# Modulation halves in the first input product: one and a half per token tile's product in place of one

## The reference, cut to what matters

```python
for l in range(DEPTH):                                  # DEPTH = 2
    mod_l = (silu_c @ w_mod[l] + b_mod[l])[:, None, :]  # (1024) @ (1024, 6144)
    mod_c = (silu_cc @ w_mod[l] + b_mod[l])[None, None, :]
    ...                                                 # split into shift, scale, gate, twice
    h_l = rmsnorm(x_lat, norm_mix_pre[l]) * (1.0 + sc1_l) + sh1_l
    h_c = rmsnorm(x_ctx, norm_mix_pre[l]) * (1.0 + sc1_c) + sh1_c
    m_l, m_c = hybrid_mixer(h_l, h_c, ...)              # h @ w_in, then attention and an SSD scan, then @ w_out
    x_lat = x_lat + g1_l * rmsnorm(m_l, norm_mix_post[l])
    ...
```

## Time and profile before

| | |
|---|---|
| time, median of 3 runs | 2771.52 us (2766.29 to 2773.17) |
| the profiled execution | 2772.69 us, its span 2771.4 us |
| PE, DVE, ACT, POOL busy | 95%, 77%, 54%, 4% of the span |
| mean granted TensorE clock | 0.969 |
| input product of layer 0 | from 40 to 175 us |
| attention and scan of layer 0 | from 175 to 316 us |

### The profile page before, as it was taken

How to read it: one execution, slowest core, us unless ns; L and a number is a source line. 1 busy time by engine, 2 the same in 40 slices (tenths; PEclk the granted TensorE clock), 3 DMA queues, 4 the chain that set the end, 5 groups by cost and what they waited for, 6 DMA issues and landing times.

```text
span 2771.4 us, 32200 instructions
## 1 busy us (share of the span) xinstructions
PE 2620.0 (95%) x12954; PEld 2132.0 (77%) x12954; DVE 2125.7 (77%) x2511; ACT 1486.9 (54%) x1665; POOL 110.6 (4%) x145
## 2 busy tenths in 40 slices
PE   7989998998998889999999999999999999999997
PEld 4767676887777678877788777788888888888886
DVE  4555566787647657868688667799999999999997
ACT  4332364445443244344633526677667776767674
POOL 4023100000000300000000000000000000000000
PEclk9999899999999989999999999999999999999999
DMA  7543545885553036952289340599999999999994
GB/s 277 183 156 122 190 166 191 299 304 203 180 210 122 1 121 240 327 197 95 96 305 328 136 175 31 185 371 364 351 367 368 353 362 365 362 354 367 369 364 189
DMA packets 290442, 675.24 MB, mean 244 GB/s; under 512 B 16726, under 2 KB 113158, under 8 KB 271344
## 3 DMA queue, kind: packets, MB, share of 16 engines
q1 hardware_dynamic: 285152, 664.35, 65.9%
q0 software_dynamic: 4272, 7.72, 1.1%
q10 hardware_dynamic: 864, 1.06, 0.1%
HBM read 671.98 MB, written 1.10 MB: 243 GB/s over the span
## 4 chain that ended last, share of the span: by engine, by line
PE 76%; DVE 13%; ACT 7%; DMA 2%; issue 1%; SPq 0%; POOL 0%; ACTq 0%; DVEq 0%; POOLq 0%
PE psum L553 21%; PE psum L555 21%; PE psum L554 21%; PE psum L76 7%; DVE wslot_r L563 3%; PE psum L1524 1%; PE psum L396 1%; ACT whi_r L76 1%; PE psum L1663 1%; DVE cacc L76 1%; PE psum L3063 1%; DVE dslot_r L563 1%; DMA first<-in_w_mod 1%; PE psum L2091 1%; DVE x L76 1%
## 5 line engine op out<-in xcount | busy, mean ns | idle before, releaser
L553 PE MATMUL psum<-whi_r,xhi_r 128*128 128x512 f32 (+1 forms) x752 | 295.5, 393 | 12.0 <-DVE wslot_r L563 5.4
L563 DVE TENSOR_TENSOR wslot_r<-wslot,whi_r 128x2048 fp32r<-128x2048 f32 (+1 forms) x114 | 255.6, 2252 | 61.5 <-ACT whi_r L76 61.1
L555 PE MATMUL psum<-whi_r,xlo_r 128*128 128x512 f32 (+1 forms) x752 | 290.4, 386 | 0.0
L554 PE MATMUL psum<-wslot_r,xhi_r 128*128 128x512 f32 (+1 forms) x736 | 283.7, 385 | 0.0
L76 ACT ACTIVATE whi_r<-wslot 128x2048 fp32r<-128x2048 f32 (+1 forms) x114 | 212.6, 1878 | 50.8 <-DMA wslot<-in_w_up 19.5
L563 DVE TENSOR_TENSOR wslot_r<-wslot,arena_r 128x2048 fp32r<-128x2048 f32 x85 | 194.0, 2288 | 18.7 <-ACT arena_r L3022 18.1
L563 DVE TENSOR_TENSOR ring_r<-ring,wide_r 128x2048 fp32r<-128x2048 f32 x84 | 191.8, 2288 | 17.8 <-ACT wide_r L3022 16.6
L563 DVE TENSOR_TENSOR wslot_r<-wslot,wide_r 128x2048 fp32r<-128x2048 f32 x83 | 189.7, 2288 | 16.7 <-ACT wide_r L3022 16.3
L563 DVE TENSOR_TENSOR ring_r<-ring,arena_r 128x2048 fp32r<-128x2048 f32 x84 | 191.6, 2287 | 11.6 <-ACT arena_r L3022 10.8
L3022 ACT ACTIVATE arena_r<-wslot 128x2048 fp32r<-128x2048 f32 x85 | 162.3, 1917 | 68.6 <-PE psum L555 45.6
L3022 ACT ACTIVATE arena_r<-ring 128x2048 fp32r<-128x2048 f32 x84 | 160.5, 1918 | 69.3 <-PE psum L555 48.5
(11 more groups left out here) (540 smaller groups left out, 6334.5 us busy)
## 6 DMA issues: line engine op xcount, KB each, us to landing
wslot<-in_moe_w_gate SPq DMA_DIRECT2D x29, 2048.0 KB, 8.0
ring<-in_moe_w_down SPq DMA_DIRECT2D x29, 2048.0 KB, 8.3
dot<-in_w_dots SPq DMA_DIRECT2D x112, 512.0 KB, 6.1
wslot<-in_moe_w_up SPq DMA_DIRECT2D x28, 2048.0 KB, 8.5
ring<-in_moe_w_up SPq DMA_DIRECT2D x28, 2048.0 KB, 8.8
ring<-in_moe_w_gate SPq DMA_DIRECT2D x27, 2048.0 KB, 8.2
wslot<-in_moe_w_down SPq DMA_DIRECT2D x27, 2048.0 KB, 8.1
dslot<-in_w_mod SPq DMA_DIRECT2D x42, 1024.0 KB, 4.8
```

The costliest lines, as they stand in the source:

```text
L553: t.matmul(out_, hi, w_hi, start=start, stop=False)
L554: t.matmul(out_, hi, w_lo, start=False, stop=False)
L555: return t.matmul(out_, lo, w_hi, start=False, stop=stop)
L563: return v.tensor_tensor(one_pass(lo), src, one_pass(hi), ALU.subtract)
```

## The change

One number: behind the products of the first layer's input, each `fill` gives 1.5 steps in place of 1.

```diff
@@ -1445,7 +1445,7 @@
                     if n + 2 < len(order):
                         fetch_tile(order[n + 2])
                 if p_ != start:
-                    fill(2)
+                    fill(3 if l == 0 else 2)
                 between(j, p_)
```

## The result

The changed kernel takes 2784.28 us in the median of 7 runs (2775.68 to 2790.76), the kernel before 2770.81 (7 runs, 2766.29 to 2773.17). The ratio is 1.0039, its 95% interval 1.0021 to 1.0057: slower by 0.4%, some 11 us, where 2781 was forecast. The profiled execution took 2778.27, 5.6 above the profiled one of before.

What follows compares the result with a forecast made beforehand. PE was taken to bound the kernel, busy for 95% of 2771.4 us. Input product +10.2, mix -4.4 and end of the mix +4.3 gave +10.1 on the median of 2771.5: 2781 us, range 2766 to 2788.

Steps and rivals of the forecast that it cites:

- `col_mod` wait and its clock gone: Input product: the 4.20 us gap ahead of the third tile's first half goes, with its low clock: -6.9 us.
- KV's pairs: Input product, around KV: paired halves wait for their transfers, n19 4.4, n20 0.3 and n23 1.0 us.
- low clock behind KV's wait: Input product: the 4.4 us wait in KV brings the clock down behind it, 0.87 + 1.85 = 2.7 us.
- input product: Stretch from 40 to 175 us: 7.05 + 0.5 - 6.9 + 9.6 = +10.2 us (8.7 to 12).
- mix to the scan's end: Stretch from 175 to 291 us: smaller gaps, less low clock and fewer waits beside attention, -4.4 us (-2.6 to -6.2).
- end of the mix, to the output product: Behind the scan's end: without its seven halves attention runs at low clock, as in layer 1: +5.1 - 0.8 = +4.3 us.
- a gap of 4.4 is as long as that of 4.20, and so I give it the same loss by the clock: Input product, KV: n19's transfer wait loses as much by the clock as the old column wait, 2.7 us.
- 1.76 + 1.1: Mix: n26 fills the 1.76 us gap at 185.44, saving 1.0; the gap at 203.30 is over about 1.1 earlier.
- I take half, 1.8: Mix: of about 3.6 us lost to low clock behind the gap at 203.30, half is saved, 1.8.
- rival B: End of the mix keeps the full clock, turning +4.3 into -7.1: -1.3 in all, 2770 us, not slower; chance 0.2.
- f: Share of the end of the mix at 2.4 GHz; the total change goes as 10.1 - 11.4 f.
- Rival C: Transfers of n19 and n20 land in time for KV's second product, 7.4 us less: +2.7, 2774 us; chance 0.13.

Runs made afterwards that it cites:

- second profile: The changed kernel run again with no edit and profiled a second time: 2787.1 us, ratio 1.0061 to the kernel before.
- asked early: The changed kernel, each half asking for the transfer of the half after next right behind its own last matmul, not at the next step: ratio 1.0022 to the kernel before.
- no transfers: The changed kernel with the transfers of n8 to n39 left out, their matmuls reading what stands in the buffers: ratio 1.0034 to the kernel before.
- filled end: The changed kernel with bursts of matmuls that nothing reads between the steps of the mix's end: ratio 1.0041 to the kernel before.
- columns early: The kernel before with two steps in place of one behind Q's last product, so the second tile's columns stand ahead of KV: 2769.92 us, ratio 0.9992.
- bare end: The kernel before with six of the seven halves behind the scan's last product left out, matmuls and transfers: ratio 1.0003.
- KV single: The changed kernel with one step behind each of KV's products, as before the change: 2776.9 us, ratio 1.0014 to the kernel before.

## Why the prediction came out nearly right

The forecast of 2781 stood on +10.1. The ratio says +10.8, the medians differ by 13.5. Its terms did not come out equally well.

| term | predicted | measured in the profile |
|---|---|---|
| more matmuls in the input product | +7.05 | as counted |
| wait behind the third tile's columns | +0.5 | 0.59, and 1.7 of low clock (second profile: 0.60 and none) |
| `col_mod` wait and its clock gone | -6.9 | gone |
| X1 pair's transfer | +1.2 | 0.44 + 1.36 - 0.93 = 0.9 |
| KV's pairs | 4.4 + 0.3 + 1.0 = 5.7 | 2.04 + 1.37 + 1.92 = 5.3 |
| low clock behind KV's wait | +2.7 | none |
| input product | +10.2 | +8.8 (second profile: +7.4) |
| mix to the scan's end | -4.4 | +1.2 |
| end of the mix, to the output product | +4.3 | -0.7 - 0.6 = -1.3 |

**The input product**: right in mechanism and, in the sum, in size. The runs bear out that waits for transfers are part of the price: asked early, 3.8 of 7.1 us of them went and the input product got 4.3 shorter; with no transfers all of them went, and 3.8 us were gained. Two sizes were off. First, the transfers behind the tile landed 2.5 us sooner than the row at 73.7 says. The buffers' view of 126 to 134 us in the kernel after:

```profile
L346 SPq DMA_DIRECT2D dslot<-in_w_mod x2: 438/540/641, 131.4 to 132.1; - x2
...
DMA to landing us min/median/max: 9.5/10.3/11.2
```

They landed 10.8 and 13.2 behind the product's end and not 13.1 and 15.3, so the first wait was 2.04. In each case 4.3 MB went through, a tile of 2 MB and two halves, and the pair's second half can't start sooner than these have landed. From 130.2 to 143.3 us the mean rate was 330 GB/s, with the core's DMA engines busy for 92% of the time, and in X1 287, from 73.6 to 88.6. The difference is in the last 0.3 MB. Up to it both went alike: 130.2 to 142.0 us, then 73.6 to 85.6, and what followed there up to 88.6:

```profile
DMA packets 1310, 4.05 MB, mean 343 GB/s; under 512 B 48, under 2 KB 48, under 8 KB 1072
```

```profile
DMA packets 1310, 4.03 MB, mean 336 GB/s; under 512 B 51, under 2 KB 51, under 8 KB 1075
```

```profile
DMA packets 47, 0.28 MB, mean 93 GB/s; under 512 B 13, under 2 KB 13, under 8 KB 13
```

In KV the rest took 1.3 us, in X1 3.0. Why that tail was slow stays open. Second, the step "a gap of 4.4 is as long as that of 4.20, and so I give it the same loss by the clock" failed with the gap: it came in two, of 2.04 and 1.37 with a half between, and the clock stayed at 1.00. (The Trainium skill, "TensorE: Matmul & The Clock Gate", section "HAM oscillation", has short bursts that each wait longer than they last for a transfer run at the low clock; the traces have it behind the waits of 2.25 and 2.38 of two other kernels, and not behind 2.24 and 2.31 in this one's second profile.) In this profile the loss came instead behind Z's columns, whose low clock the prediction had passed over: 2.05 us of 8-column matmuls, 0.59 of idling, and 3.4 us at 0.51. In the second profile it came nowhere, and in the filled end, the same program up to there, behind KV's pair as forecast, for 6.1 us. So which stall of this stretch pays by the clock is not a thing that the order settles; the three input products took 143.8, 142.4 and 144.5 us.

Also mis-stated, though it didn't enter the sum, was that -6.9 is there for the taking: columns early got 4.8 of it, as Z's split is next. In the kernel after the pairs of halves covered that split.

**The mix to the scan's end**: this is the term that failed. PE's idle time there fell by 3.0 us (117.00 - 105.94 against 115.80 - 101.76), as 1.76 + 1.1 said. But PE was busy 4.2 us longer with work that is equal by count (16.1 us each), at a clock of 0.91 against 0.93. The step "I take half, 1.8" took the low clock at 203 as tied to its gap: with the gap gone, the low clock moved to 212, 222 and 232. The clock of this stretch isn't a property of the order: five profiles with after's order of it have 117.0, 119.0, 113.1, 118.8 and 113.0 us, at clocks of 0.91, 0.90, 0.94, 0.90 and 0.95. Their mean of 116.2 is 1.1 above that of the two profiles with before's order (115.8, and 114.4 in the bare end). I should have written the term as 0 with 3 to either side.

**The end of the mix**: predicted +4.3 on a low clock throughout, measured -1.3, with 13.7 of its 24.7 us at 0.50 and the rest at 1.00. Between the forecast and rival B, in its own formula: f is 0.45 by the share of time (11.0 of 24.7). The formula gives 4.3 - 11.4 x 0.45 = -0.8, which is near. What the runs add is that the price is real (bare end: 30.9 us with six of seven halves out), and that how much of it is paid differs from profile to profile: 24.7, 24.6, 24.8, 27.6 in four with after's order of it. Rival B's rule of the Trainium skill ("TensorE: Matmul & The Clock Gate", section "Why this matters for your kernels") asks, to keep the rate, only that PE have no long idle gaps. The traces do not agree in general: with no gap over 0.69 between them, the same transposes and values ran at 0.50 from 294.2 to 320.2 in the bare end, and at 1.00 from 314.8 in after.

**The sum** met the median since two errors of opposite sign, 5.6 in the mix and 5.6 in the end, cancelled, and since the runs as a whole ran at a lower clock than the profiled execution (0.964 against 0.968), whose time their median exceeds by 6.0. In the profiled execution itself it is 5.6 against a forecast of 10.1: 8.7 up to the output product, of which 3.1 came back behind 330 us, where the prediction had put nothing. So the direction rests on the input product, and the closeness of the number is luck. That the loss at large is the input product's is argued from equal-clock runs (+8) and from the stretches (+8.8 and +7.4), with the bare end to show that the work had cost nothing where it stood. No kernel undid the loss alone: asking early removed only half of the waits, and the kernel with KV single came to 1.0014, but at a higher mean clock.

Rival C was wrong in its price as well as its premise: with no transfers at all the loss was still 0.34%, not 0.1%, in part because DVE's next wait and its low clock took what they left, and at a mean clock of 0.964 against 0.967.

## What to carry to other kernels

Work that is laid between the units of a stage that waits from unit to unit can cost nothing there, and may even hold PE's clock up; moved into a full stage it costs its whole length. The busy share does not tell the two apart: PE was busy for 95% of both stretches here. Ask what the stage would take without the work. When buffered loads are consumed in pairs in place of one at a time, their wait is set by what stands ahead of them in the queue: write down the bytes ahead, and ask for the next load behind the last reader, not at the next step. And if a stall goes, list what is second in the queue of the engine that caused it: here the split behind the same norm took back 2.06 of 6.9 us. With both moved the kernel was measurably faster, with one it was not, though the intervals of the two overlap.

## What the runs showed of the hardware

The length of a wait did not tell whether low clock followed. Waits of 2.25, 2.38 and 2.45 us had halves of 1.70, 1.56 and 1.94 behind them; waits of 2.24 and 2.31 in the second profile of after had halves of 1.07, and one of 2.06 in columns early left the clock at 1.00. A wait of 0.59 behind 8-column matmuls had a half of 1.94 behind it in one profile of after and of 1.07 in the other. Which instruction meets the low clock is not fixed by the program. The same kernel had 0.89 and 0.95 over the same stretch in two profiles. Over the runs the time follows the mean granted clock, in after from 2775.68 us at 0.968 to 2797.43 at 0.959, in a program whose work does not change. And less work can come at a lower clock: leaving out 6 us of matmuls changed the time of the whole by nothing that could be measured.
